# A two-layer hybrid decoder trunk on one core: roots by Sqrt and reciprocal in the mixers, table loads placed by hand, a new order of ScalarE and VectorE, and another layout of the split tokens

## What is computed

```python
def hybrid_mixer(x, w_in, conv_w, v_g, v_b, w_s, b_s, out_g, w_out):
    proj = x @ w_in
    b_gate, c_gate, h, u, v = jnp.split(proj, [...], axis=-1)        # five times 512 columns
    y_conv = b_gate * causal_short_conv(c_gate * h, conv_w)
    y_sg = chunked_spatial_gating(gelu(u), gelu(v), v_g, v_b, w_s, b_s)
    y = jnp.concatenate([head_rms_norm(y_conv, 8, 64), head_rms_norm(y_sg, 4, 128)], axis=-1) * out_g
    return y @ w_out

def head_rms_norm(y, n_heads, head_dim):
    yf = y.reshape(bsz, s, n_heads, head_dim)
    yf = yf * lax.rsqrt(jnp.mean(jnp.square(yf), axis=-1, keepdims=True) + RMS_EPS)
    ...

for i in range(DEPTH):
    mix = hybrid_mixer(x, ...)
    x = layer_norm(ALPHA * x + mix, ln1_g[i], ln1_b[i])
    ffn = swiglu(x, ...) if i % 2 == 0 else moe_swiglu(x, ...)       # 2816 wide; 8 experts of 3584, top 2
    x = layer_norm(ALPHA * x + ffn, ln2_g[i], ln2_b[i])
```

## Time and profile before

| | us |
|---|---|
| median of 3 runs | 1372.63 (1370.7 to 1374.06) |
| the profiled execution | 1371.43 |
| its span | 1369.7 |
| PE busy | 1351.3 |
| DVE busy | 1130.5 |
| ACT busy | 923.5 |

### The profile page before, as it was taken

How to read it: one execution, slowest core, us unless ns; L and a number is a source line. 1 busy time by engine, 2 the same in 40 slices (tenths; PEclk the granted TensorE clock), 3 DMA queues, 4 the chain that set the end, 5 groups by cost and what they waited for, 6 DMA issues and landing times.

```text
span 1369.7 us, 16433 instructions
## 1 busy us (share of the span) xinstructions
PE 1351.3 (99%) x6825; PEld 1144.5 (84%) x6825; DVE 1130.5 (83%) x829; ACT 923.5 (67%) x715; POOL 22.3 (2%) x36
## 2 busy tenths in 40 slices
PE   9999999999999999999999999999999999999996
PEld 9978888889788888888888888888888888888885
DVE  5876555587689899889989988898998889889886
ACT  5565444444777777777777777777777777777773
POOL 0000000020000000000000000000000000000000
PEclk9999999999999999999999999999999999999998
DMA  9937555555459999999999999999999999999991
GB/s 327 351 123 237 193 185 184 190 180 190 149 204 395 377 373 360 353 359 362 358 369 374 367 353 361 360 358 359 374 365 357 356 362 369 359 372 378 355 379 59
DMA packets 202643, 425.86 MB, mean 311 GB/s; under 512 B 7828, under 2 KB 51908, under 8 KB 202564
## 3 DMA queue, kind: packets, MB, share of 16 engines
q1 hardware_dynamic: 201456, 421.06, 86.2%
q0 software_dynamic: 1024, 3.67, 0.9%
q10 hardware_dynamic: 84, 0.02, 0.0%
HBM read 423.68 MB, written 1.05 MB: 310 GB/s over the span
## 4 chain that ended last, share of the span: by engine, by line
PE 93%; DVE 3%; ACT 3%; issue 1%; DVEq 0%; POOL 0%; POOLq 0%; ACTq 0%
PE turn L1285 17%; PE turn L1287 17%; PE turn L1286 17%; PE accp L1285 9%; PE accp L1286 9%; PE accp L1287 9%; PE turn L1366 3%; PE turn L1363 3%; PE accp L1585 2%; PE turn L1365 1%; PE turn L1364 1%; PE accp L1612 1%; DVE w_lo L764 1%; PE accp L1571 1%; ACT w_hi L467 1%
## 5 line engine op out<-in xcount | busy, mean ns | idle before, releaser
L764 DVE TENSOR_TENSOR w_lo<-raw,w_hi 128x2048 fp32r<-128x2048 f32 (+1 forms) x401 | 907.0, 2269 | 152.8 <-ACT w_hi L467 148.6
L467 ACT CAST w_hi<-raw 128x2048 fp32r<-128x2048 f32 x395 | 756.0, 1916 | 217.7 <-PE turn L1287 114.7
L1285 PE MATMUL turn<-w_hi,a_hi 128*128 128x512 f32 x664 | 262.6, 395 | 0.4 <-DVE w_lo L764 0.4
L1287 PE MATMUL turn<-w_hi,a_lo 128*128 128x512 f32 x664 | 259.1, 390 | 0.0
L1286 PE MATMUL turn<-w_lo,a_hi 128*128 128x512 f32 x664 | 258.7, 390 | 0.0
L1285 PE MATMUL accp<-w_hi,hT_hi 128*128 128x512 f32 x448 | 175.0, 391 | 0.0
L1286 PE MATMUL accp<-w_lo,hT_hi 128*128 128x512 f32 x448 | 174.5, 390 | 0.0
L1287 PE MATMUL accp<-w_hi,hT_lo 128*128 128x512 f32 x448 | 174.3, 389 | 0.0
L1287 PEld LDWEIGHTS turn<-w_hi,a_lo 128*128 128x128 f32 x664 | 124.6, 188 | 26.6
L1285 PEld LDWEIGHTS turn<-w_hi,a_hi 128*128 128x128 f32 x664 | 124.8, 188 | 25.3 <-DVE w_lo L764 0.8
L1286 PEld LDWEIGHTS turn<-w_lo,a_hi 128*128 128x128 f32 x664 | 124.9, 188 | 24.6
(11 more groups left out here) (231 smaller groups left out, 1558.2 us busy)
## 6 DMA issues: line engine op xcount, KB each, us to landing
raw<-in_we_gate SPq DMA_DIRECT2D x112, 1024.0 KB, 7.5
raw<-in_we_up SPq DMA_DIRECT2D x112, 1024.0 KB, 7.6
raw<-in_we_down SPq DMA_DIRECT2D x112, 1024.0 KB, 7.4
raw<-in_w_in SPq DMA_DIRECT2D x18, 1024.0 KB, 6.1
raw<-in_w_gate SPq DMA_DIRECT2D x11, 1024.0 KB, 5.4
raw<-in_w_up SPq DMA_DIRECT2D x11, 1024.0 KB, 5.4
raw<-in_w_down SPq DMA_DIRECT2D x11, 1024.0 KB, 5.0
raw<-in_w_out SPq DMA_DIRECT2D x8, 1024.0 KB, 8.4
```

Of the source, the lines that this page charges most:

```text
L467: nc.scalar.copy(w_hi[:, p % PARTS, :], raw[:, p % RING, :]).then_inc(hi_done, 1)
L764: return nc.vector.tensor_tensor(out, whole, hi.bitcast(f32), ALU.subtract)
L1285: nc.tensor.matmul(to, lh, rh, start=start, stop=False, **group)
L1287: return nc.tensor.matmul(to, ll, rh, start=False, stop=stop, **group)
```

## The change

Four edits.

1. `roots` does one activation, Sqrt, on each half, and `over_rms` on DVE does a reciprocal of 128x512 ahead of its two products, and waits for it. The semaphore between Ln and Exp goes.
2. `preload_act_table` places table loads: Gelu at ACT's start, Sqrt behind the split of `at+11`, Gelu behind the conv roots, Sqrt behind the gated squares, Silu before the dense layer, Gelu before layer 1, Exp and Silu in the routing.
3. The order: the split of `at+12` goes behind `round_y` on ACT and behind the z additions on DVE; the z additions go behind the conv half's `rest_of_y` on DVE; the split of `at+13` goes behind `roots` on ACT and behind `over_rms` on DVE; the splits of `at+14` and `at+15` go behind both remainders.
4. `t_both` alternates the parts: for each block of 128 channels the 256 high values and then the 256 low ones, so that the wide matmul reads 512 values in a run. The token-major view of the same buffer that the experts read keeps its layout.

```diff
-        t_both = sb("t_both", [P, 2, KD * TOK], f32r)
+        t_both = sb("t_both", [P, 2 * KD * TOK], f32r)
...
-        xT_both = t_both[:, :, :].rearrange("p i (k t) -> p k i t", k=KD)
+        xT_both = t_both[:, :].rearrange("p (k i t) -> p k i t", k=KD, i=2)
+        xT_hi, xT_lo = (xT_both[:, :, i, :] for i in range(2))
+        xT_pair = t_both[:, :].rearrange("p (k t) -> p k t", k=KD)
...
@@ ACT, each layer @@
-                splits(at + 11, at + 12)
+                split_hi(at + 11)
+                nc.scalar.preload_act_table(ACT.Sqrt)
...
                         nc.scalar.activation(buf[:, 2 * i:2 * i + 2, :], means[:, 2 * i:2 * i + 2, :],
-                                             ACT.Ln, bias=eps_rms).then_inc(rms_log, 1)
-                    for i in range(2):
-                        act.wait_ge(rms_log, 4 * l + 2 * group + i + 1)
-                        nc.scalar.activation(buf[:, 2 * i:2 * i + 2, :], buf[:, 2 * i:2 * i + 2, :], ACT.Exp,
-                                             scale=-0.5).then_inc(rms_ready, 1)
+                                             ACT.Sqrt, bias=eps_rms).then_inc(rms_ready, 1)
...
                 roots(0, conv_mean, acc_half[:, 0:4, :], conv)
+                nc.scalar.preload_act_table(ACT.Gelu)
                 round_y(0, 0)
                 round_y(0, 1)
+                split_hi(at + 12)
...
+                nc.scalar.preload_act_table(ACT.Sqrt)
+                roots(1, gmlp_mean, turn_half[:, 4:8, :], zb2)
                 split_hi(at + 13)
-                roots(1, gmlp_mean, turn_half[:, 4:8, :], zb2)
                 round_y(1, 0)
-                split_hi(at + 14)
                 round_y(1, 1)
-                split_hi(at + 15)
+                splits(at + 14, at + 15)
...
@@ DVE, each layer @@
-                splits(at + 11, at + 12)
+                split_lo(at + 11)
...
                         dve.wait_ge(rms_ready, 4 * l + 2 * group + i + 1)
+                        step(nc.vector.reciprocal(buf[:, 2 * i:2 * i + 2, :], buf[:, 2 * i:2 * i + 2, :]))
...
@@ PE @@
-                        nc.tensor.matmul(whole, wh[:, k, at], xT_both[:, k], start=(k == 0), stop=False)
+                        nc.tensor.matmul(whole, wh[:, k, at], xT_pair[:, k, :], start=(k == 0), stop=False)
```

More of the change, by code:

```diff
@@ L89, in hybrid_trunk_kernel @@
         x = sb("x", [P, NT, D])
-        t_both = sb("t_both", [P, 2, KD * TOK], f32r)
-        t_hi, t_lo = t_both[:, 0], t_both[:, 1]
+        t_both = sb("t_both", [P, 2 * KD * TOK], f32r)
         a_hi = sb("a_hi", [P, KD * TOK], f32r)
@@ L153, in hybrid_trunk_kernel @@
         centred = y_work[:, :].rearrange("p (n d) -> p n d", n=NT)
-        xT_hi, xT_lo, y_hi, y_lo = (
-            a.rearrange("p (k t) -> p k t", k=KD) for a in (t_hi, t_lo, a_hi[:, :], a_lo[:, :]))
-        xT_both = t_both[:, :, :].rearrange("p i (k t) -> p k i t", k=KD)
-        x_hi, x_lo = (a.rearrange("p (n d) -> p n d", n=NT) for a in (t_hi, t_lo))
+        y_hi, y_lo = (a[:, :].rearrange("p (k t) -> p k t", k=KD) for a in (a_hi, a_lo))
+        xT_both = t_both[:, :].rearrange("p (k i t) -> p k i t", k=KD, i=2)
+        xT_hi, xT_lo = (xT_both[:, :, i, :] for i in range(2))
+        xT_pair = t_both[:, :].rearrange("p (k t) -> p k t", k=KD)
+        x_both = t_both[:, :].rearrange("p (i n d) -> p i n d", i=2, n=NT)
+        x_hi, x_lo = (x_both[:, i] for i in range(2))
         xg_hi, xg_lo = ([two[:, 0], two[:, 1], third[:]] for two, third in (
@@ L236, in hybrid_trunk_kernel @@
             sem(n) for n in ("gate_copied", "gate_summed", "up_copied", "up_summed"))
-        conv_mean, gmlp_mean, rms_log, rms_ready, y_normed, y_hi_ready, y_ready = (
-            sem(n) for n in ("conv_mean", "gmlp_mean", "rms_log", "rms_ready", "y_normed", "y_hi_ready", "y_ready"))
+        conv_mean, gmlp_mean, rms_ready, y_normed, y_hi_ready, y_ready = (
+            sem(n) for n in ("conv_mean", "gmlp_mean", "rms_ready", "y_normed", "y_hi_ready", "y_ready"))
         sum_done, ln_var, ln_rstd, ln_norm = (sem(n) for n in ("sum_done", "ln_var", "ln_rstd", "ln_norm"))
@@ L561, in _ @@
                     round_tile(1, 1)
+                    nc.scalar.preload_act_table(ACT.Silu)
                     for j in range(GROUPS):
@@ L610, in _ @@
             split_hi(MOE_AT + 3)
+            nc.scalar.preload_act_table(ACT.Exp)
             for b in range(4):
@@ L972, in rest_of_y @@
                     rest_of(y_lo[:, c:c + 2, :], y[:, c:c + 2, :], y_hi[:, c:c + 2, :]).then_inc(y_ready, 1)
+                dve.wait_ge(y_conv_raw, 2 * l + 2)
+                over_rms(0, conv)
+                rest_of_y(0, 0)
+                rest_of_y(0, 1)
                 dve.wait_ge(bs_loaded, 16)
@@ L982, in _ @@
                 last.then_inc(zb_ready, 1)
[L983 to L986, removed]
+                split_lo(at + 12)
                 dve.wait_ge(zb_ready, l + 1)
@@ L992, in _ @@
                                             zb2[:, 2 * i:2 * i + 2, :], ALU.mult).then_inc(y_gmlp_raw, 1)
-                split_lo(at + 13)
                 dve.wait_ge(y_gmlp_raw, 2 * l + 2)
                 over_rms(1, zb2)
+                split_lo(at + 13)
                 rest_of_y(1, 0)
-                split_lo(at + 14)
                 rest_of_y(1, 1)
-                split_lo(at + 15)
+                splits(at + 14, at + 15)
                 if l == 0:
@@ L1360, in two_wide_blocks @@
                     at = slice(b * P, (b + 1) * P)
-                    whole, first = to[:, b, :].rearrange("p (i t) -> p i t", i=2), to[:, b, 0:TOK]
+                    whole, first = to[:, b, :], to[:, b, 0:TOK]
                     for k in range(0, KD, 2):
-                        nc.tensor.matmul(whole, wh[:, k, at], xT_both[:, k], start=(k == 0), stop=False)
+                        nc.tensor.matmul(whole, wh[:, k, at], xT_pair[:, k, :], start=(k == 0), stop=False)
                         nc.tensor.matmul(first, wl[:, k, at], xT_hi[:, k, :], start=False, stop=False)
                         nc.tensor.matmul(first, wl[:, k + 1, at], xT_hi[:, k + 1, :], start=False, stop=False)
-                        last = nc.tensor.matmul(whole, wh[:, k + 1, at], xT_both[:, k + 1], start=False,
+                        last = nc.tensor.matmul(whole, wh[:, k + 1, at], xT_pair[:, k + 1, :], start=False,
                                                 stop=(k == KD - 2))
```

## The result

The changed kernel takes 1389.81 us in the median (1389.14 to 1391.21, 4 runs), beside 1371.66 us for the kernel before (4 runs): 1.0132 times as long, 95% interval 1.0114 to 1.0149, 18 us more. The profiled execution took 1389.75 us, its span 1387.9.

A forecast was written before the change was run, and what follows sets the result against it. PE was taken as the bound, busy 99%, so mixer changes show only as its stalls. Chain 15.6 plus clock 2.6 minus layout 0.3 gave 17.9 us on 1371.43 or 1372.63, so 1390, range 1377 to 1400.

The forecast's parts named there:

- The price of R: Time of a DVE reciprocal of 128x512, priced from one 128x2 row 5 to 6 ns above its neighbours: 3.4 us.
- The eight passes: Rival: the reciprocal divides iteratively with repeat count 8, taking 4.3 to 4.4 us; about 1398 us, chance 0.20.
- The conv half: Mixer's first root chain: reciprocals delay PE's first y piece in layer 0 from 71.91 to 75.8, 3.9 us late.
- The gated half: Mixer's second root chain, layer 0: third y piece at 93.6, last at 96.4 where it was 88.59.
- 4R - 5.8: Loss per layer in us, R being the reciprocal's time: 7.8 at R = 3.4, gain and loss parting at R = 1.45.
- The clock: PE's granted clock falling behind the mixer stalls: 1.3 us a layer, 2.6 in all, between 0 and 3.4.
- the fall behind the second stall: Clock fall after PE's wait for a_lo late in each mixer: up to 1.7 us, 1.3 a layer taken.
- the fall behind the first stall: Clock fall after PE's wait for the z additions: claimed covered by the second stall, so costing nothing.
- The sum: 15.6 for the chain in two layers plus 2.6 for the clock minus 0.3 for the layout: 17.9 us.
- The table loads: 11 instead of 15 on ACT, 1.28 us each; moved ones stand where ACT waits, cost and gain zero.
- The layout: 304 wide matmuls of the dense layer reading 512 contiguous values: 0.3 us won, bounds 0 and 1.5.
- The rival of the plain pass: The reciprocal costs one plain DVE pass, 0.6 us: stalls shrink, 1368 us, faster by 0.33%; chance 0.19.

The follow-up runs named there:

- e9_fill_both: Changed kernel with unused matmuls filling both TensorE stalls in each mixer (17 before the z additions' wait, 14 ahead of last_rows): 1384.22 us, 1.0107 of before.
- e1_pass: Changed kernel with each 128x512 reciprocal replaced by one VectorE pass (times 1.0), the inverse left out: 1365.66 us, 0.9964 of before.
- e2_half: Changed kernel with the reciprocal taken over only one of the two 256-wide channel blocks of each half: 1371.46 us, 1.0006 of before.
- e6_fill: Changed kernel with 14 unused matmuls ahead of last_rows in each mixer, filling only the second TensorE stall: 1385.36 us, 1.0106 of before.
- e10_loads_alone: Kernel before with only table loads changed: one set holding Ln and Exp loaded early, Gelu behind the conv roots: 1365.68 us, 0.9966 of before.
- e3_lnexp: Changed kernel with Ln and Exp in place of Sqrt and reciprocal, Exp's load still between them: 1369.9 us, 0.9994 of before.

## Why the prediction held, step by step

The forecast was 1390 and the measured median 1389.81. The sign, the mechanism and both places were right; the two large terms were off in opposite directions, so part of that nearness is luck.

- **The price of R.** 3.4 taken, 3.35 measured. The reading that the second element alone shows the pace (5.5 ns more) was near the 6.24 - 1.04 = 5.2 ns measured. It rested on 5 ns of one row.
- **The eight passes** that the Trainium skill, page "VectorE: DVE Perf Modes", section "First, the fixed hardware budget", states would have made 4.3 us by the prediction's estimate; 3349 ns at 512 and 1749 at 256 are six times 1.04 ns an element. The measurement decides.
- **The conv half.** First y piece at 75.8, measured 75.48.
- **The gated half.** Third y piece at 93.6 and last at 96.4, measured 94.21 and 98.65. With the stalls filled they come at 92.92 and 95.81, so the chain was a little shorter than put down, and the lateness is the clock's.
- **The slope.** Starts of layer 0's norm against 90.66: +0.73 at R = 1.75 and +7.12 at R = 3.35 (clock at 1.00 in both), that is 4.0 us per us of R, as in 4R - 5.8. The constant is -6.3 instead of -5.8; the times that I added up along the chain were a little too long. So the chain costs 7.1 us a layer, not 7.8, and the point where it turns is R = 1.57.
- **The clock** was under-sized. I had 2.6 us. From the changed kernel to e9_fill_both it is 1389.8 - 1384.2 = 5.6 us, 4.4 by the second stall's filling and 1.1 by the first's. The larger part of the miss is the fall behind the second stall, sized at 1.3 us a layer after the one in the earlier trace rows; in layer 1 the low clock lasted longer. The smaller is the argument that the fall behind the first stall is covered by the second stall. This step failed in layer 0: the means go through the slowed PE, and ACT waited 1.31 us for them; in layer 1 it held. The medians of different sets of runs are compared here, so each of the two has some tenths of doubt.
- **The sum.** Chain 15.6 predicted. Measured 14.2 in the two mixers, and 14.0 from the medians of e9_fill_both and of before beside it. With the clock's 5.6 that makes 19.6 us, 1.7 more than the 17.9 of the sum, and it counts from a before of 1370.2. The forecast counted from 1371.43 and 1372.63, and the before of the result is at 1371.66. So the low sum and the high start cancelled too: being right to 0.2 us is luck.
- **The start.** The profile of before has the fall of the clock in the routing, 1.7 us. Those of the changed kernel, e1_pass, e2_half, e6_fill, e9_fill_both and e10_loads_alone don't have it, the other four do. The profiled run of e3_lnexp, which has it, took 1372.17 beside a median of 1369.9. So it seems to come in some executions and not in others, and may be part of the spread of before; in which of its runs it is no trace shows.
- **The table loads** are 11 of 1283 ns. That of the conv half is hidden, as put down (0.79 us of wait behind it). That of the gated half stands in the chain, as the sum had it, wherever the means aren't late: in layer 1 of the changed kernel, and in e9_fill_both. The drain that the Trainium skill, page "ScalarE: Activation LUTs", section "What ACT_TABLE_LOAD costs", adds to a load shows in no row: in e9_fill_both the load starts at 79.53, 0.02 us behind the squares, and Sqrt at 80.82, 0.01 us behind the load.
- **The layout**: 0.3 put down, 0 by the rows and none in the medians.
- **The rival of the plain pass** put 1368 on a single pass; e1_pass gave 1365.66, 5.1 us below its before where 4.2 + 0.3 was worked out. That case would have been a clear gain, not one at the edge.

## What to carry to other kernels

Price an operation at the size at which it will run: one of 128x2 told of the reciprocal at 128x512 only by 5 ns, and a chain that passes through it four times before it feeds a busy TensorE hands on every microsecond four times, once its slack is used up (here above R = 1.57). If a root must be inverted on a tile of this size, two activations of one table set (0.6 us each) were cheaper here than a root and a reciprocal, once the set that holds both is loaded in a wait. And when a chain starts to make TensorE wait for several microseconds, look for the clock behind each stall too, and for the engines that wait for the slowed TensorE.

## What the runs showed of the hardware

- RECIPROCAL in f32 on VectorE takes 3349 ns for 128x512, 1749 for 128x256 and 167 for 128x2: 6.24 ns an element, six times TENSOR_TENSOR's 1.04, over a fixed part like that of the others.
- The granted clock fell to 0.50 behind idle stretches of TensorE of 4.1 and 3.1 us in the mixers of this kernel, and stayed at 1.00 behind stretches of 0.9 us and less (e2_half). With the long stretches filled by matmuls without use it stayed at 1.00 too. Such filling took 4.4 to 5.6 us off a kernel that had lost its feed.
- A float32r matmul whose 512 moving values are two runs of 256 is shown with the same 395 to 396 ns as one with a single run, and its follower starts the same 0.23 us later.
- TENSOR_SCALAR in place on 128x512 f32 took 423 ns for one multiplication by an immediate, against 547 in the earlier trace rows for two operations with scalars from memory.
